# The last output projection with token blocks stationary, and the last norm on token rows

## What is computed

```python
def odd_mixer(h, w_in, conv_w, conv_b, ln_g, ln_b, w_out):
    a, b, g = jnp.split(h @ w_in, 3, axis=-1)          # 2048 -> 3 x 4096
    u = a * jax.nn.sigmoid(b)
    u = dwconv(u, conv_w) + conv_b
    u = jax.nn.silu(layernorm(u, ln_g, ln_b))
    return (u * jax.nn.silu(g)) @ w_out                # 4096 -> 2048
...
        h_p = y_p * (1.0 + sc_c) + sh_c
        h_s = y_s * (1.0 + sc_s) + sh_s
...
        y_p = layernorm(ALPHA * y_p + gt_c * o_p, ln_g[l], ln_b[l])
        y_s = layernorm(ALPHA * y_s + gt_s * o_s, ln_g[l], ln_b[l])
```

## Times and profile before

| | us |
|---|---|
| median of 3 runs | 2566.84 |
| lowest, highest | 2565.62, 2566.97 |
| span of the profiled execution | 2565.9 |
| PE busy in it | 2515.2 |
| DVE, ACT, POOL busy | 1959.0, 934.7, 922.9 |
| last projection on PE, from its first start to the end of its last matmul | 2278.2 to 2546.4 |
| from there to the end of the span | 19.5 |

### The profile page before, as it was taken

The page is one execution under the profiler, slowest core; times in us unless marked ns, Lnnn a source line. Parts: engine busy times, 40 slices in busy tenths (PEclk is TensorE's granted clock), DMA queues, the critical chain, the costliest instruction groups (busy, mean ns, idle before and its releaser), DMA issues.

```text
span 2565.9 us, 40433 instructions
## 1 busy us (share of the span) xinstructions
PE 2515.2 (98%) x14486; PEld 2467.1 (96%) x14486; DVE 1959.0 (76%) x3411; ACT 934.7 (36%) x1232; POOL 922.9 (36%) x618
## 2 busy tenths in 40 slices
PE   6999999999999999999999999999999999999997
PEld 3699999999999999999999999999999999999997
DVE  2488888989888888889643389999999999484213
ACT  1233333333333333334322354333333333463223
POOL 0111111110111111111344566666666666572444
PEclk9999999999999999999999999999999999999998
DMA  9975666555565556565444334444343443564332
GB/s 387 347 214 189 200 193 198 184 195 197 193 209 195 191 184 199 189 200 161 155 147 139 129 111 136 138 138 130 126 137 129 135 129 130 180 208 131 124 125 89
DMA packets 131567, 442.02 MB, mean 172 GB/s; under 512 B 16720, under 2 KB 27216, under 8 KB 131456
## 3 DMA queue, kind: packets, MB, share of 16 engines
q1 hardware_dynamic: 114912, 409.23, 46.8%
q0 software_dynamic: 7328, 18.71, 3.6%
q10 hardware_dynamic: 9216, 12.59, 1.5%
HBM read 423.03 MB, written 15.18 MB: 171 GB/s over the span
## 4 chain that ended last, share of the span: by engine, by line
PE 90%; DVE 5%; DMA 3%; issue 1%; ACT 1%; POOL 1%; SPq 0%; ACTq 0%; DVEq 0%; POOLq 0%
PE bank L508 29%; PE bank L510 29%; PE bank L509 29%; DMA map<-in_w_ada_dram 2%; DVE w_lo L404 1%; PE bank L607 1%; PE bank L524 1%; DMA raw<-in_w_ada_dram 1%; DVE vk L1127 1%; DVE x L1317 0%; DVE part L1032 0%; ACT w_hi L725 0%; DVE o_lo L1176 0%; POOL w_lo L404 0%; DVE probT L1149 0%
## 5 line engine op out<-in xcount | busy, mean ns | idle before, releaser
L508 PE MATMUL bank<-h_hi,w_hi 128*128 128x384 f32 x3543 | 1191.9, 336 | 4.9 <-DVE h_lo L970 2.3
L510 PE MATMUL bank<-h_hi,w_lo 128*128 128x384 f32 x3543 | 1184.6, 334 | 0.0
L509 PE MATMUL bank<-h_lo,w_hi 128*128 128x384 f32 x3543 | 1184.3, 334 | 0.0
L725 ACT ACTIVATE w_hi<-raw 128x1024 fp32r<-128x1024 f32 x572 | 595.4, 1058 | 867.7 <-PE bank L510 611.4
L404 POOL TENSOR_TENSOR w_lo<-raw,w_hi 128x1024 fp32r<-128x1024 f32 x247 | 603.8, 2462 | 544.6 <-ACT w_hi L725 542.3
L508 PEld LDWEIGHTS bank<-h_hi,w_hi 128*128 128x128 f32 x3543 | 665.6, 188 | 22.8 <-issue 12.6
L509 PEld LDWEIGHTS bank<-h_lo,w_hi 128*128 128x128 f32 x3543 | 665.7, 188 | 0.6
L510 PEld LDWEIGHTS bank<-h_hi,w_lo 128*128 128x128 f32 x3543 | 665.5, 188 | 0.0
L404 DVE TENSOR_TENSOR w_lo<-raw,w_hi 128x1024 fp32r<-128x1024 f32 x325 | 396.4, 1236 | 257.9 <-ACT w_hi L725 244.8
L1393 DVE SCALAR_TENSOR_TENSOR bank<-up,cw,bank 128x399 f32<-128x399 f32 x896 | 487.0, 627 | 0.0
L508 PE MATMUL bank<-o_hi,w_hi 128*128 128x384 f32 x1024 | 343.1, 335 | 1.7 <-DVE w_lo L404 1.0
(11 more groups left out here) (188 smaller groups left out, 1526.5 us busy)
## 6 DMA issues: line engine op xcount, KB each, us to landing
raw<-in_w_in_even_dram SPq DMA_DIRECT2D x256, 512.0 KB, 4.2
raw<-in_w_in_odd_dram SPq DMA_DIRECT2D x192, 512.0 KB, 3.3
raw<-in_w_ada_dram SPq DMA_DIRECT2D x120, 512.0 KB, 4.2
map<-in_w_ada_dram SPq DMA_DIRECT2D x64, 512.0 KB, 13.5
raw<-in_w_out_even_dram SPq DMA_DIRECT2D x64, 512.0 KB, 3.9
raw<-in_w_out_odd_dram SPq DMA_DIRECT2D x64, 512.0 KB, 3.3
gates<-sg ACTq DMA_DIRECT2D x32, 192.0 KB, 1.9
lg<-gates ACTq DMA_DIRECT2D x32, 192.0 KB, 3.8
```

The source lines that it names most:

```text
L508: pe.matmul(out, w_hi[slot][:, t, :], hi[:, kk, :], start=(kk == 0), stop=False)
L509: pe.matmul(out, w_hi[slot][:, t, :], lo[:, kk, :], start=False, stop=False)
L510: mm = pe.matmul(out, w_lo[slot][:, t, :], hi[:, kk, :], start=False, stop=last)
L725: act.activation(w_hi[mine][:], raw[slot][:], ACT.Copy).then_inc(hi_ready, 1)
```

## The change

The orientation of OUT1 is turned. `o_hi` and `o_lo` of one block of channels and 128 tokens are now stationary, and 512 output channels of weights move; the sums stand with tokens on the partitions, in banks 0, 1, 2 for even chunks of 512 channels and 3, 5, 6 for odd ones. Slabs of `w_out_odd` hold two blocks of k by 512 channels. There are four chunks, each of 16 slabs; in the last chunk the last four slabs are gone through once per token block, so that the three blocks end one after the other.

For that x has to stand with tokens on the partitions too. During `ODD`, behind slabs 9, 11, ... 39, PE transposes block t of x (three 128x128 transposes into bank 5), and ACT copies it back times ALPHA. The sums over tokens (`pivot_sum`, squares, `total`, `energy`, `token_moments`) are gone from OUT1: DVE multiplies the bank by the gate row, adds it to x, and takes `bn_stats` of each tile of 128 x 512; for chunks 0 to 2 POOL multiplies by g beside it. After the last chunk DVE closes each token block: `bn_aggr`, root on ACT, reciprocal, shift; chunks 0 to 2 by DVE, chunk 3 by ACT and POOL. SP stores 12 tiles of 256 KB in place of 16 of 192 KB.

Gates, g and b are needed as rows, the same on all partitions. ACT's queue stores the gate columns as a line to DRAM (two DMAs, runs of one element) in pair 2 of `ODD`, loads it broadcast (2 MB) in the norm stage, and g and b (1 MB each) in body 0 of OUT1. They lie over buffers that are free by then.

```diff
@@ SP @@
-                for r, (_, s, _) in enumerate(OUT1.order):
-                    load(OUT1, i, r, slab_of(OUT1, r, w_out_odd, i * 4 + s))
+                for r in range(OUT1.nraw):
+                    load(OUT1, i, r, w_out_odd[ds(i, 1), r].rearrange("s p f -> (s p) f"))
+            for n in range(TILES):
+                for i in range(OUT1.bodies):
...
+                    sp.dma_start(y[n * P:(n + 1) * P, i * WIDE:(i + 1) * WIDE].rearrange("p (a b) -> p a b", b=P),
+                                 tile_chunk(i, n)).then_inc(y_stored, 16)
@@ PE @@
+            def turn_input(t):
+                pe.wait_ge(x_ready, t + 1)
+                if t:
+                    pe.wait_ge(x_turned, t)
+                for n in range(TILES):
+                    ins = pe.transpose(bank[B_S0][:, n * P:(n + 1) * P], x[:, t, n * P:(n + 1) * P], eye)
+                ins.then_inc(x_tiles_ready, 1)
+            def tile_step(i, k, half, n):
...
+                pe.matmul(out[:], o_hi[:, c, mine], high, start=(c == 0), stop=False)
+                pe.matmul(out[:], o_hi[:, c, mine], low, start=False, stop=False)
+                return pe.matmul(out[:], o_lo[:, c, mine], high, start=False, stop=(c == KE - 1))
+            def tile_projection():
+                for i in range(OUT1.bodies):
+                    if i == 0:
+                        for b in TILE_BANKS[0]:
+                            pe.wait_ge(bank_free[b], OUT1.bank(0, b)[1])
+                    elif i == 1:
+                        pe.wait_ge(bank_free[3], OUT1.bank(0, 3)[1])
+                    else:
+                        pe.wait_ge(chunk_ready, TILES * (i - 1))
+                    last = i == OUT1.bodies - 1
+                    for k in range(BY_TILE if last else OUT1.nw):
...
+                        for half in range(2):
+                            if i == 0:
+                                pe.wait_ge(osplit_ready, KE + 2 * k + half + 1)
+                            for n in range(TILES):
+                                mm = tile_step(i, k, half, n)
...
+                for n in range(TILES):
+                    for k in range(BY_TILE, OUT1.nw):
+                        if not n:
+                            odd, ready = OUT1.low(OUT1.bodies - 1, k)
+                            pe.wait_ge(lo_ready[odd], ready)
+                        for half in range(2):
+                            mm = tile_step(OUT1.bodies - 1, k, half, n)
+                    mm.then_inc(tile_done, 1)
...
+                if k % 2 and 0 <= k // 2 - 4 < KD:
+                    turn_input(k // 2 - 4)
@@ ACT @@
+                if 5 <= n < KD + 5:
+                    act.wait_ge(x_tiles_ready, n - 4)
+                    act.activation(x[:, n - 5, :], bank[B_S0][:, 0:T], ACT.Copy, scale=ALPHA).then_inc(x_turned, 1)
+                if n == 2:
+                    act.wait_ge(gate_known, 1)
+                    for c in range(2):
+                        act.dma_start(gate_line[c].rearrange("(t p) -> p t", p=P), mod[:, 5, :, c], allow_slow_non_contiguous=True)\
+                           .then_inc(gate_stored, 16)
...
+                    act.dma_start(gate_rows[:], gate_line.rearrange("(o c) d -> o c d", o=1).partition_broadcast(P))\
+                       .then_inc(gate_rows_landed, 16)
...
+                for n in range(TILES):
+                    act.wait_ge(var_known, n + 1)
+                    act.activation(deviation[:, n:n + 1], tile_mean_var[:, n, 1:2], ACT.Sqrt, bias=eps[:])\
+                       .then_inc(deviation_known, 1)
+                    act.wait_ge(shift_known, n + 1)
+                    chunk = tile_chunk(SHIFTED_BY_DVE, n)
+                    act.activation(chunk, chunk, ACT.Identity, bias=shift_tile[:, n:n + 1],
+                                   scale=rstd_tile[:, n:n + 1]).then_inc(scaled_out, 1)
@@ DVE @@
+                def gated(i, n):
...
+                    dve.tensor_tensor(made_tile, made_tile, gate_rows[:, min(n, 1), i * WIDE:(i + 1) * WIDE], ALU.mult)\
...
+                    dve.tensor_tensor(chunk, chunk, made_tile.rearrange("p (a b) -> p a b", b=P), ALU.add)\
...
+                    dve.bn_stats(chunk_stats[:, n, 6 * i:6 * i + 6], chunk).then_inc(chunk_counted, 1)
+                def normalised(n):
...
+                    dve.bn_aggr(tile_mean_var[:, n, :], chunk_stats[:, n, :]).then_inc(var_known, 1)
+                    dve.wait_ge(deviation_known, n + 1)
+                    dve.reciprocal(rstd_tile[:, n:n + 1], deviation[:, n:n + 1]).then_inc(rstd_tile_ready, 1)
...
+                    for i in range(SHIFTED_BY_DVE):
+                        dve.scalar_tensor_tensor(bank[TILE_BANKS[0][i]][:], g_row[:, i * WIDE:(i + 1) * WIDE],
+                                                 shift_tile[:, n:n + 1], b_row[:, i * WIDE:(i + 1) * WIDE],
+                                                 ALU.mult, ALU.add).then_inc(shifted, 1)
+                    for i in range(SHIFTED_BY_DVE):
...
+                        dve.scalar_tensor_tensor(chunk, chunk, rstd_tile[:, n:n + 1], bank[TILE_BANKS[0][i]][:]
+                                                 .rearrange("p (a b) -> p a b", b=P), ALU.mult, ALU.add).then_inc(applied, 1)
...
+                for n in range(TILES):
+                    gated(OUT1.bodies - 1, n)
+                    normalised(n)
@@ POOL @@
+                def weighted(i, n, done, count):
+                    chunk = tile_chunk(i, n)
+                    pool.tensor_tensor(chunk, chunk, row_chunk(g_row, i), ALU.mult).then_inc(done, 1)
...
+                for n in range(TILES):
+                    pool.wait_ge(scaled_out, n + 1)
+                    weighted(SHIFTED_BY_DVE, n, weighted_last, n + 1)
+                    chunk = tile_chunk(SHIFTED_BY_DVE, n)
+                    pool.tensor_tensor(chunk, chunk, row_chunk(b_row, SHIFTED_BY_DVE), ALU.add).then_inc(applied_last, 1)
```

More of the change, by code:

```diff
@@ L187 @@
 POOLED = KD - 1
[L188 to L195 removed]
+CALLS = (POOLED, KE - 2)
+BEFORE = (0, KD)
+CLEARED = (1, 2 + POOLED)
 class Steps:
@@ new lines, in tile_step @@
+            def tile_step(i, k, half, n):
+                c = 2 * k + half
+                out, slot = bank[TILE_BANKS[i % 2][n]], OUT1.w(0, k) % RING
+                high, low = (w[slot][:].rearrange("p t n -> p (t n)")[:, half * WIDE:(half + 1) * WIDE] for w in (w_hi, w_lo))
+                mine = slice(n * P, (n + 1) * P)
+                pe.matmul(out[:], o_hi[:, c, mine], high, start=(c == 0), stop=False)
+                pe.matmul(out[:], o_hi[:, c, mine], low, start=False, stop=False)
+                return pe.matmul(out[:], o_lo[:, c, mine], high, start=False, stop=(c == KE - 1))
@@ L1544, in body @@
                             low_half(pool, ph, i, 2 * pair + 3)
-                        if first and layer:
-                            odd_step(PAIRS_ODD + pair)
                         for t in ADDED.get((i, pair), ()):
                             if t < POOLED:
-                                add_with_square(2 * layer, t, x, z_ready, KD * layer)
-                        if ends and not last:
+                                add_with_square(0, t, x, z_ready, 0)
+                        if ends:
```

261 lines of the change are left out of this document (155 added, 106 removed).

## The result

| | before | after |
|---|---|---|
| median of the runs, us | 2567.16 (2564.04 to 2571.18) | 2573.3 (2571.82 to 2575.52) |
| ratio, 95% interval | | 1.0022 (1.0013 to 1.003) |
| span of the profiled execution | 2565.9 | 2571.3 |
| last projection on PE, first start to end of last matmul | 2278.16 to 2546.43, 268.3 | 2290.60 to 2551.98, 261.4 |
| last matmul to the end of the span | 19.5 | 19.3 |

The change costs 6.1 us by the medians, where -1.8 was forecast, and the time lies 0.3 us above the range. The projection gained what was forecast and 1.2 us more; what was to come from the tail did not come, and some 4.7 us were lost in a place priced at 0.7. h_hi and h_lo are the halves of the input of `ODD`, o_hi and o_lo those of the input of the last projection.

A forecast was written before the change was run, and what follows sets the result against it. TensorE, busy 98% of the span, was taken as the bound. Terms -5.1 + 5.2 - 0.6 + 2.7 + 0 - 4.7 + 0.7 = -1.8 gave a span of 2564.1, a median forecast of 2565.0 us, range 2552 to 2573.

The forecast's parts named there:

- The projection itself: Last projection on PE: 1152 matmuls of 512 columns in place of 1536 of 384, -5.1 us, ends 0 and -16.6.
- (a): Reading of the projection's pace: 13.3 ns extra per matmul with its weight load, 226.7 ns each, -5.1 us; chance 0.43.
- Transposes and pivot: On PE: 48 added transposes during the odd projection at 0.108 us each, +5.2 us; one pivot sum removed, -0.6 us.
- The start: Start of the last projection: PE waits for bank 2, which ScalarE reads out late, +2.7 us.
- the upper end of 5.3: Start of the projection: about 5.3 us if the granted clock falls in the gap and some 5 us run at half pace.
- Chunks 0 to 2, the ring: VectorE and GpSimd work beside the projection's matmuls, and slab 15's slot in the last chunk: cost 0, at most 0.5 us.
- DMAs on ScalarE's queue: Row loads cost 0, up to 2 us; the gate store early in ODD holds ScalarE's queue, +0.7 us.
- Rival 3: Store of single elements holds ScalarE's queue early in ODD, 9.3 us in place of 0.7: 2573.6 us, slower; chance 0.10.
- around 1507 no wait of PE over 1 us: Sign for the forecast, near slab 8 of ODD: the gate store makes PE wait no more than 1 us.
- The tail: After the last matmul: three tiles of 7.2 us on VectorE, end at E + 14.8 against 19.5, -4.7 us.
- a tenth on all operations as a bound: Tail's slow end: wide operations at 0.75, slowed a tenth by GpSimd's work, a tile 8.3 us, term -1.4 us.
- the other bound, -5.6: Tail's fast end: all nine wide VectorE operations of a tile at 0.66 us, term -5.6 us.

The follow-up runs named there:

- a3: The changed kernel with one wait added, so GpSimd starts its chunk 3 product only after VectorE's three shifts of that token block: 2572.4 us.
- b1: The changed kernel with the gate columns turned on TensorE and stored later, as 32 runs of 512 bytes: 2570.0 us.
- a1: The kernel before with only the two stores of 4-byte runs added at pair 2 of ODD: 2572.2 us.
- f3: The changed kernel with turned gates, other banks and GpSimd's wait for the shifts, plus three unread GpSimd operations behind its last: 2568.8 us.
- f2: The changed kernel with turned gates, other banks and GpSimd's wait for the shifts, plus the last tile's chunk 3 closed by VectorE: 2560.9 us.
- a4: The changed kernel with other banks for the tiles, so the first tile matmul does not wait for bank 2: 2568.9 us.
- b4: The changed kernel with one transpose per block of x in place of three: 2568.9 us.
- b2: The kernel before with 256 columns a matmul in its last projection, run once for its trace: matmul starts 0.120 us apart.
- a2: The changed kernel with the gate store moved from pair 2 to pair 40 of ODD: 2569.0 us.
- d1: The changed kernel with turned gates, other banks and GpSimd's wait for the shifts, plus last stores taken from gate rows in one run: 2564.7 us.

## Why the prediction was wrong, step by step

**The projection itself: right.** (a) is an extra of 32 cycles for each matmul: 226.7 forecast, 226.7 measured, and 120.0 at the third width. Whether it is paid for the load, as the prediction supposed, stays open. A further 1.2 us came from two waits for o_lo that the kernel before had, and this is not in the sum.

**Transposes and pivot: right.** +5.2 and -0.6 forecast; by the traces -0.65, and +4.8 for 14 of the 16 groups, some 5.4 for all.

**The start: right in its mechanism and in size.** 2.7 forecast, 2.3 found, and the upper end of 5.3, for a granted clock that falls in the gap, is what the profiles of a3 and b1 show in part. The median may say that I should have kept more of that end in the sum: taking the wait away brought 4.7, with 3.3 to either side.

**Chunks 0 to 2, the ring: right**, at nothing.

**DMAs on ScalarE's queue: the step that failed first.** I asked how long the issue holds ACT's queue, and got that right (2.04 us against 1.8), and what it costs PE nearly so (a wait of 0.97 against 0.7). I did not ask what 4096 runs of 4 bytes do in the DMA engines, which every slab of weights passes through too; that was put at nothing, and it is the second wait, 1.90, with the fall of the clock behind it. The sum has 0.7 where it should have had 4.7 (a1). Rival 3 had the right place, the right sign and nearly the right total (2573.6), by a mechanism that did not occur: the queue was not held for 10 us. The forecast sentence "around 1507 no wait of PE over 1 us" was the test; the trace has 0.97 at 1509, which passes it, and the 1.90 stands at 1524, where that sentence did not look.

**The tail: the step that failed second.** -4.7 forecast, -0.15 found. The list of operations and all but one of their durations are right. The first part missed is the 1.0 us per tile for which L1477 stands behind GpSimd, with 0.1 more for small steps: VectorE ends at E + 14.05, not E + 10.7. I had put a tenth on all operations as a bound, and a tile of 8.3 us came out of that by luck (the other bound, -5.6, should be about -5.8 by its own rows); the cause was one operation of nine. The second part is the last line of that step: "from the last operation's end to the end of the span it is 4.0 us now, and I keep that". It was the wrong operation. The 4.0 us stood behind VectorE's last; what held was the 6.1 behind GpSimd's (f3, f2). In the changed kernel GpSimd does its last work late in the last tile, E + 13.2, so the end could not come before E + 19.3, whatever the stores did. a3 parts the two: there VectorE ends at E + 11.0, close to the forecast, and the tail is still 17.9. So of the 4.5 us that the tail missed, 1.4 are the operation that stands behind GpSimd and 3.1 the end that was hung on the wrong engine.

Of the 7.9 us between -1.8 and +6.1, the store is 4.0 and the tail 4.5; all the rest, the clock behind h_lo and a projection 1.2 better than forecast among it, comes to about -0.6, inside the intervals.

What stays open: why the clock fell behind the 1.7 us wait at 1487.5 in the profiles of the changed kernel, of a3 and b1, and not in the other eleven traces, which have the same wait; why it fell behind the wait for w_lo near 1524 in the changed kernel (1.90 us) and a4 (2.6), and not in a1 (1.7), b4 (1.9) and a3 (2.4); how often it falls at the start of the projection; and why GpSimd's DRAIN takes 5.89 us.

## What to carry to other kernels

A transfer has two prices, the time its issue holds a queue and the time its runs fill the engines that all queues share; bytes tell of neither, so a store of single elements belongs where no load is awaited, or is turned first. When a wait has two possible causes, follow each one back to what its engine stood for: two waits of the same name here had different ones. Ask of an end which engine closes last and not only which transfer lands last: here what lay behind GpSimd's last operation was a fixed 6.1 us, so its work belongs before the last stretch. When work is put beside other work, look at where the sources of both stand, not only at how busy the engines are.

## What the runs showed of the hardware

- fp32r matmuls with a load each start 120.0, 173.3 and 226.7 ns apart at 256, 384 and 512 columns (b2, before, after): columns at 2.4 GHz plus 13.3 ns. A plain fp32 transpose of 128x128 among them adds 0.105 us (b4).
- Two stores of 2048 runs of 4 bytes (8 KB each) took 16 to 17 us to land, the median of the two (after, a1, a2); slabs of 512 KB issued in that time took 12.3 to 13.7 us in place of 3.3. Their issue held the queue for 1.3 to 2.0 us. The same data as 32 runs of 512 bytes landed in 1.4 us (b1).
- A VectorE operation with both sources in SBUF (0.76 us) took 1.8 us when GpSimd (1.26 us alone, 1.65 then) came in before it; one with a source in PSUM was not changed (after, a3).
- In thirteen traces the span ended 6.09 to 6.17 us after GpSimd's last operation, in one with GpSimd done early (f2) 10.9 us after it and 1.05 us after the last store's traffic. GpSimd's closing DRAIN ended 5.89 us behind its last operation in all fourteen.
- Stores of 256 KB, several under way, ran at some 290 GB/s in runs of 512 bytes (after), at some 355 in runs of 2 KB (d1).
